# First layer's gate tiles as three pairs of seven quarter products; modulation steps four in a row

## What is computed

```python
for l in range(DEPTH):                                   # DEPTH = 2
    shift, scale, gate = jnp.split(sc @ w_ada[l] + b_ada[l], 3, axis=-1)   # modulation
    hc = rms_norm(h_ctx, norm_g[l]) * (1.0 + scale_c) + shift_c
    pc = split_cols(hc @ w_in[l])                        # context stream, layer 0
    hx = rms_norm(x, norm_g[l]) * (1.0 + scale[:, None, :]) + shift[:, None, :]
    px = split_cols(hx @ w_in[l])                        # q, k, v, gates, conv, fourier inputs
    attn = windowed_attention(q, k, v, kc, vc, attn_sink[l])
    y = jnp.concatenate([attn * silu(g_att), y_conv * silu(g_conv), y_four * silu(g_four)], -1) @ w_out[l]
    x = x + gate[:, None, :] * y
```

## Time and profile before

| | us |
|---|---|
| median of 3 runs (lowest, highest) | 1026.42 (1026.13, 1026.56) |
| profiled execution | 1026.29 |
| its span | 1024.5 |
| TensorE busy | 1000.3 (98%) |
| VectorE busy | 512.5 (50%) |
| ScalarE busy | 354.5 (35%) |
| GpSimd busy | 85.9 (8%) |
| first layer's attention | 145.65 to about 242 |

### The profile page before, as it was taken

One profiled execution on the slowest core, in us unless ns is written; L12 is line 12 of the kernel. 1 busy time (PEld: TensorE's weight loads), 2 busy tenths in 40 slices (PEclk: granted clock), 3 DMA queues, 4 the chain that ended last, 5 costly groups with the idle time before them and its releaser, 6 DMA issues.

```text
span 1024.5 us, 15340 instructions
## 1 busy us (share of the span) xinstructions
PE 1000.3 (98%) x5676; PEld 710.9 (69%) x5676; DVE 512.5 (50%) x1398; ACT 354.5 (35%) x861; POOL 85.9 (8%) x140
## 2 busy tenths in 40 slices
PE   6999999999999999999999999999999999999996
PEld 2458554556887777988999877899999744444442
DVE  5459836447365667566865824853534510000004
ACT  5224133435043247245475134742121411111113
POOL 0061000032200004300000000000000010000000
PEclk9999999999999999999999999999999999999999
DMA  9972124762233422364354352058647799999996
GB/s 362 420 303 95 42 82 178 291 272 83 83 123 130 158 83 70 130 236 139 115 202 163 126 202 83 2 195 328 237 186 307 295 396 420 419 422 420 421 419 248
DMA packets 34518, 227.57 MB, mean 222 GB/s; under 512 B 4641, under 2 KB 4913, under 8 KB 9200
## 3 DMA queue, kind: packets, MB, share of 16 engines
q1 hardware_dynamic: 31360, 214.97, 53.4%
q10 hardware_dynamic: 1920, 9.80, 2.5%
q0 software_dynamic: 1168, 1.85, 0.5%
HBM read 222.15 MB, written 8.41 MB: 225 GB/s over the span
## 4 chain that ended last, share of the span: by engine, by line
PE 90%; DVE 6%; DMA 2%; ACT 1%; issue 1%; SPq 0%; DVEq 0%; ACTq 0%
PE lin L669 12%; PE sc L686 11%; PE lin L1398 11%; PE sc L792 6%; PE aux L1398 5%; PE lin L686 4%; PE aux L1246 4%; PE sc L892 4%; PE lin L856 3%; PE sc L1363 3%; PE sc L669 3%; PE aux L922 3%; PE sc L1071 3%; PE lin L908 2%; DVE UN L2284 2%; DMA Y<-ada_in 2%
## 5 line engine op out<-in xcount | busy, mean ns | idle before, releaser
L669 PE MATMUL lin<-H,ring 128*128 128x256 f32 (+1 forms) x560 | 125.8, 385 | 0.0
L669 PEld LDWEIGHTS lin<-H,ring 128*128 128x128 f32 x560 | 106.0, 190 | 18.0 <-issue 4.2
L792 PE MATMUL sc<-H,ring 128*128 128x512 f32 (+1 forms) x192 | 67.3, 496 | 0.0
L1614 ACT ACTIVATE SP<-lin 128x512 f32<-128x512 f32 (+2 forms) x88 | 42.0, 485 | 72.7 <-PE lin L908 72.6
L2284 DVE SCALAR_TENSOR_TENSOR UN<-UN,cols 128x512 f32<-128x512 f32 (+1 forms) x120 | 66.7, 627 | 0.0
L2196 DVE CUSTOM_DVE_ANT_0 SP<-sc,CW,SK 128x512 f32<-128x512 f32 (+1 forms) x48 | 31.8, 662 | 53.6 <-PE sc L892 53.6
L1625 ACT ACTIVATE SP<-SP,ST 128x513 f32<-128x513 f32 (+4 forms) x88 | 53.8, 611 | 6.7 <-DVE ST L2199 6.4
L792 PEld LDWEIGHTS sc<-H,ring 128*128 128x128 f32 x192 | 34.8, 189 | 30.3 <-issue 25.6
L2851 DVE TENSOR_TENSOR PR<-lin,PR 128x512 f32<-128x512 f32 x8 | 5.5, 692 | 94.5 <-PE lin L1398 94.5
L892 PE MATMUL sc<-PR 64*128 64x256 f32 (+3 forms) x240 | 42.2, 434 | 2.3 <-DVE ST L2196 1.5
L1246 PE MATMUL aux<-Y,ring 128*128 128x256 f32 x192 | 42.0, 379 | 0.2 <-DVE PR L2645 0.2
(11 more groups left out here) (503 smaller groups left out, 1867.6 us busy)
## 6 DMA issues: line engine op xcount, KB each, us to landing
ring<-w_stream SPq DMA_DIRECT2D x119, 1024.0 KB, 6.7
SP<-w_stream SPq DMA_DIRECT2D x14, 1024.0 KB, 20.3
UN<-w_stream SPq DMA_DIRECT2D x10, 1024.0 KB, 18.2
PR<-w_stream SPq DMA_DIRECT2D x8, 1024.0 KB, 17.0
CW<-w_stream SPq DMA_DIRECT2D x8, 1024.0 KB, 16.4
X<-w_stream SPq DMA_DIRECT2D x8, 1024.0 KB, 18.7
Y<-w_stream SPq DMA_DIRECT2D x8, 1024.0 KB, 18.2
PR<-ada_in SPq DMA_DIRECT2D x5, 1024.0 KB, 26.4
```

The source lines that it names most:

```text
L669: m = mm(dst, w[:, k, :], rhs(k), start=n == 0, stop=n == KT - 1)
L792: m = mm(bank[:, 0:ns * SEQ], filling["w"][:, k, :], H[:, 0:ns, k, :], start=k == 0, stop=k == KT - 1)
L1614: fn(PT[:, g % TURNED, a:b], take()[:, 0:b - a], ACT.Copy).then_inc(lin_taken, 1)
```

## The change

The six gate tiles of the first layer are computed as three pairs, each by seven quarter products, as the paired tiles of the opening are. One step of the attention carries one quarter product (four products of 256 columns): 21 steps instead of 24. Each quarter lands in one of two PSUM banks by turns (`fill_bank`) and VectorE reads it there, by 9 operations of 256 columns for each pair; ScalarE's six copies are gone. A product waits until the quarter two before it has been read. The weights of a pair are one unit, which is given back after the seventh product.

The token mixtures must live on: the fourth is written to other space (where the conv's inputs stand, so after these have been used), GpSimd copies the first after its third weight mixture and the second when the last tile of both streams is done. GpSimd mixes the weights of the first gate pair before the attention, and those of the second and third ahead of the sinks of items 14 and 28. The four steps of a modulation chunk stand in a row (steps 7 to 10 and 20 to 23). The load of the kept memory moves from step 32 to 35, and `S_OUT` uses other space.

```diff
-FILLS = ([("gate", 0), ("gate", 1), ("ada", 1), ("gate", 2), ("gate", 3), ("ada", 2), ("gate", 4), ("gate", 5)],
-         [("gate", t) for t in range(GATES)])
-SEQUENCE = (("gate", 0, 0, 4), ("ada", 1, 0, 2), ("gate", 1, 0, 4), ("ada", 1, 2, 2), ("gate", 2, 0, 4), ("ada", 2, 0, 2),
-            ("gate", 3, 0, 4), ("ada", 2, 2, 2), ("gate", 4, 0, 4), ("gate", 5, 0, 4))
+FILLS = ([("ada", 1), ("ada", 2)], [("gate", t) for t in range(GATES)])
+GATE_PAIRS = GATES // 2
+SEQUENCE = (("gate", 0, 0, 7), ("ada", 1, 0, 4), ("gate", 1, 0, 7), ("ada", 2, 0, 4), ("gate", 2, 0, 7))
 GATES_FROM = ADA_BLOCKS + sum(len(f) for f in FILLS)
-PIECES = ([(what, x, 2 * q) for what, x, a, n in SEQUENCE for q in range(a, a + n)],
+PIECES = ([(what, x, q if what == "gate" else 2 * q) for what, x, a, n in SEQUENCE for q in range(a, a + n)],
           [("gate", t, 4 * q) for t in range(GATES) for q in range(2)])
-FILL_STEPS = ([*PIECES[0][:30], None, *PIECES[0][30:]],
+FILL_STEPS = ([*PIECES[0][:11], None, *PIECES[0][11:14], None, *PIECES[0][14:26], None, PIECES[0][26], None, *PIECES[0][27:]],
...
-OUT_PART, B_PART = 7 * 3, 7 * 11
+F_PART, F_ADDED, F_MIX, F_TOKENS = 7 * 3, 3 * 3, 3, 4
...
-        T_IN = [T_IN[:, q, :, :] for q in range(4)]
+        T_IN = [*(T_IN[:, q, :, :] for q in range(3)), E1[:, 1024:2048].rearrange("p (k n) -> p k n", k=4)]
+        T_FILL = [E1[:, 0:1024].rearrange("p (k n) -> p k n", k=4), H[:, 1, 0:4, :], T_IN[2], T_IN[3]]
+        S_FILL = [E1[:, QUARTER * VV:QUARTER * (VV + 1)], *(CW[:, N_C1 + QUARTER * q:N_C1 + QUARTER * (q + 1)] for q in range(2))]
         T_OUT = SP[:, 4 * 772:].rearrange("p (q k n) -> p q k n", q=3, k=4)
         T_OUT = [FT, *(T_OUT[:, q, :, :] for q in range(3))]
         T_OUT = [T_OUT, [YB[:, k:k + 4, 1, a:a + P] for k in (0, 4) for a in (0, P)]]
...
+        def fill_bank(q):
+
+            return sc[:, q % 2, 512:512 + SEQ]
+
...
+                        if layer == 0:
+                            pe.wait_ge(quarter_added, F_ADDED + 7 * GATE_PAIRS)
...
+            def gate_quarter(x, q):
+
+                n, (lo, hi), (s1, s2, s4), (t1, t3, t2, t4) = 7 * x + q, LO_HI, S_FILL, T_FILL
+                if q == 0:
+                    assert at["block"] // UNIT == FILL_UNIT[x]
+                    filling["w"] = unit_of_pair()
+                w = filling["w"]
+                if n == 0:
+                    pe.wait_ge(four_taken, 2)
+                if q == 0:
+                    pe.wait_ge(quarter_added, F_ADDED + n)
+                if q == 1 and x:
+                    pe.wait_ge(fill_taken, ADA_BLOCKS + x)
+                if q >= 2:
+                    pe.wait_ge(quarter_added, F_ADDED + n - 1)
+                if q == 0:
+                    m = quarter(fill_bank(q), w[:, 0, lo], H[:, 0, 0:4, :])
+                if q == 1:
+                    m = quarter(fill_bank(q), w[:, 0, hi], H[:, 0, 4:8, :])
+                if q == 2:
+                    pe.wait_ge(weights_mixed, 4 * (F_MIX + x) + 1)
+                    pe.wait_ge(tokens_mixed, F_TOKENS + 1)
+                    m = quarter(fill_bank(q), s1, t1)
+                if q == 3:
+                    pe.wait_ge(weights_mixed, 4 * (F_MIX + x) + 3)
+                    m = quarter(fill_bank(q), s2, t2)
+                if q == 4:
+                    pe.wait_ge(tokens_mixed, F_TOKENS + 2)
+                    m = quarter(fill_bank(q), w[:, 1, lo], t3)
+                if q == 5:
+                    pe.wait_ge(weights_mixed, 4 * (F_MIX + x) + 4)
+                    m = quarter(fill_bank(q), s4, H[:, 1, 4:8, :])
+                if q == 6:
+                    m = quarter(fill_bank(q), w[:, 1, hi], t4)
+                    at["owed"] += 1
+                m.then_inc(quarter_made, 1)
+
             def fill(layer, i):
                 ns = 2 - layer
-                if i < len(FILL_STEPS[layer]) and FILL_STEPS[layer][i]:
-                    what, x, k0 = FILL_STEPS[layer][i]
+                step = FILL_STEPS[layer][i] if i < len(FILL_STEPS[layer]) else None
+                if layer == 0 and step and step[0] == "gate":
+                    gate_quarter(*step[1:])
+                elif step:
+                    what, x, k0 = step
                     n, b, taken = fill_of(layer, what, x)
                     bank = sc[:, b, 512:1024]
                     if k0 == 0:
                         pe.wait_ge(fill_taken, taken)
-                        if n in (ADA_BLOCKS, ADA_BLOCKS + 2):
-                            pe.wait_ge(four_taken, b + 1)
+                        if layer == 0:
+                            pe.wait_ge(quarter_added, F_ADDED + 7 * x - 1)
                     if what == "ada":
                         m = ada_step(bank, k0)
                     else:
...
+                    if layer == 0 and what == "gate":
+                        return
...
-                    if layer == 0 and i == len(FILL_STEPS[0]) - 1:
-                        memory_again()
                     if i == 2 * (len(STAGES[L]) // 2):
                         act.wait_ge(fill_taken, ADA_BLOCKS + len(FILLS[0]) + layer * len(FILLS[1]))
                     for k in gate_steps.get(i, ()):
+                        if k == 4 and layer == 0:
+                            act.wait_ge(quarter_added, F_ADDED + 7 * GATE_PAIRS)
+                            memory_again()
                         if k == 4:
                             act.wait_ge(conv_norm, layer + 1)
...
+            pool.wait_ge(tokens_mixed, F_TOKENS)
+            nc.gpsimd.tensor_copy(T_FILL[0], T_IN[0]).then_inc(tokens_mixed, 1)
+            pool.wait_ge(quarter_made, F_PART)
+            pool.wait_ge(four_ready, 2)
+            mixed(F_MIX, FILL_UNIT[0], *LO_HI, S_FILL)
+            pool.wait_ge(lin_ready, turn["l0", GF + 1] + 1)
+            pool.wait_ge(tokens_mixed, F_TOKENS + 1)
+            nc.gpsimd.tensor_copy(T_FILL[1], T_IN[1]).then_inc(tokens_mixed, 1)
             pool.wait_ge(sinks_ready, 1)
+            mixed_before = {14: 1, 28: 2}
             for name in ("l0", "l1"):
                 for i, it in enumerate(STAGES[name]):
                     g = first[name] + i
+                    if g in mixed_before:
+                        x = mixed_before[g]
+                        pool.wait_ge(quarter_made, F_PART + 7 * x - 1)
...
                 layer = int(name == "l1")
                 if layer:
                     pool.wait_ge(normed["l1"], 2 * KT)
+                else:
+                    pool.wait_ge(conv_norm, 1)
+                    pool.wait_ge(roped, 5)
                 for n in range(4):
                     if n == 2:
-                        pool.wait_ge(tokens_mixed, 4 * layer + 8)
-                    mixed(len(PAIRED) + 4 * layer + n, FIRST_OUT[layer] + n, *LO_HI[::-1], S_OUT[4 * layer + n])
+                        pool.wait_ge(tokens_mixed, OUT_TOKENS + 4 * layer + 4)
...
-                    dve.wait_ge(tokens_mixed, 3)
-                    v.tensor_tensor(T_IN[3], H[:, 0, 4:8, :], T_IN[2], ALU.subtract).then_inc(tokens_mixed, 1)
...
+                if layer == 0:
+                    after(last[1])
+                    dve.wait_ge(tokens_mixed, 3)
+                    v.tensor_tensor(T_IN[3], H[:, 0, 4:8, :], T_IN[2], ALU.subtract).then_inc(tokens_mixed, 1)
...
+                def gate_quarter(x, q):
+
+                    n, added = 7 * x + q, F_ADDED + 7 * x
+                    bank, (c11, c12), (c21, c22) = fill_bank(q), *([P1[:, GA + 2 * x + f, s, :] for s in range(2)] for f in range(2))
+                    dve.wait_ge(quarter_made, F_PART + n + 1)
+                    if q == 0:
+                        v.tensor_copy(c12, bank).then_inc(quarter_added, 1)
+                    if q == 1:
+                        dve.wait_ge(quarter_added, added + 1)
+                        v.tensor_tensor(c11, c12, bank, ALU.add).then_inc(quarter_added, 1)
+                    if q == 2:
+                        v.tensor_copy(c22, bank).then_inc(quarter_added, 1)
+                    if q == 3:
+                        v.tensor_tensor(c12, c12, bank, ALU.add).then_inc(quarter_added, 1)
+                    if q == 4:
+                        dve.wait_ge(quarter_added, added + 4)
+                        v.tensor_tensor(c21, c12, bank, ALU.add).then_inc(quarter_added, 1)
+                        step(v.tensor_tensor(c12, c12, c22, ALU.add))
+                        dve.wait_ge(quarter_added, added + 5)
+                        joined_at[0] = step(v.tensor_tensor(c22, c22, c21, ALU.add))
+                    if q == 5:
+                        after(joined_at[0])
+                        v.tensor_tensor(c12, c12, bank, ALU.add).then_inc(quarter_added, 1)
+                    if q == 6:
+                        v.tensor_tensor(c21, c21, bank, ALU.add).then_inc(quarter_added, 1)
+
+                joined_at = [0]
+
                 def between(p):
+                    for i in (2 * p, 2 * p + 1):
```

(3 more changed lines are left out.)

31 lines of the change are left out of this document (18 added, 13 removed).

## The result

The changed kernel takes **1042.65 us**, median of four runs (1041.38 to 1045.08), against 1026.37 for the kernel before (1026.13 to 1026.56): a ratio of 1.0162, 95% interval 1.0143 to 1.018. The direction was predicted, the size was not: +7.3 us were forecast and +16.3 came, and 1042.65 lies 3.65 us above the range's upper end. The profiled execution is the fastest of the four (1041.38 us, span 1039.6); its span is 15.1 us longer than that of before. The trace is of that run, so the 15.1 is what can be placed.

What follows compares the result with a forecast made beforehand. TensorE was taken to bound the kernel. Gate products -5.2, ring waits +8.6 and VectorE's lateness +3.9 gave +7.3 us, so 1033.7 us, with a range of 1028.5 to 1039.

Steps and rivals of the forecast that it cites:

- What bounds the kernel: First layer: TensorE is busy 98% of the span, so each microsecond of its instructions or new waits moves the end.
- The gain of the gate products: First layer's attention: 21 quarter-product steps replace 24 gate steps, 37.4 us for 42.6, so TensorE has 5.2 us less.
- Ring waits: Attention's modulation steps, four in a row: TensorE waits for weight units, 8.6 us in sum, bounds 7.9 and 11.
- R1: Modulation steps: units are there in time, leaving -5.2 + 3.9 = -1.3 us, 1025.1 us; chance 0.08.
- The fourth mixture and the port: Before the conv: moved mixture and GpSimd's lock on the shared port make VectorE, then TensorE, 3.9 us late; bounds 1.2, 5.2.
- the rival without a lock: Before L1019, with only the fourth mixture moved: GpSimd does not hold VectorE, wait 1.5 us; no chance given.
- R2: Before L1019: VectorE's lateness does not reach TensorE, leaving -5.2 + 8.6 = +3.4 us, 1029.8 us; chance 0.14.
- R3: Neither ring waits nor VectorE's lateness cost TensorE anything, leaving -5.2 us, 1021.2 us; chance 0.05.
- What lies beside other work: Mostly attention: VectorE's 27 sums, the conv's norm, weight mixtures and ScalarE's copies put at 0, bounds -0.3 and +3 us.
- R4: Attention: VectorE's sums set the pace and each product waits for the sum two steps back, 1039 us; chance 0.11.
- The sum: Whole kernel: -5.2 + 8.6 + 3.9 = +7.3 us, which later stages keep; 1033.7 us, chance 0.62.

Runs made afterwards that it cites:

- e_turn_five: Changed kernel with early fourth mixture, modulation steps apart, units freed sooner, second modulation turn before gate sums, five useless products in step 26's ring wait: 1025.73 us.
- e_busy: Changed kernel with useless products filling TensorE's waits before L1068 and before the waiting modulation steps: 1037.42 us, ratio 1.0106 to the kernel before.

## Why the prediction was wrong, point by point

**What bounds the kernel**: right. Every wait of TensorE in the first layer, and every product less, reached the end.

**The gain of the gate products**: right, 4.9 us measured for 5.2 forecast. The forecast took the 13 groups of the kernel before for the late first product of a group; the 21 new steps stand in 18 groups, and 5 x 0.09 is the half microsecond by which 37.9 exceeds 37.4. `e_turn_five` shows that the gain is real: its attention takes 96.6 us (145.59 to 242.14) instead of 97.1, with 2.43 us of useless products and 1.6 us of ring waits in it.

**Ring waits**: right in place and size. Forecast 3.1 + 1.2 + 4.3 = 8.6; measured 3.50, 1.45 and 4.16, 9.1 in all. The unit of the first group's fourth step was said to land 6.6 us after the third step starts, 5.5 after its issue; it was issued 1.2 us after that start (176.2), as forecast, and landed 6.2 us after its issue. That of the second group was to land 5.9 us after the third step's start, and the fourth could start 6.1 us after it (221.01 to 227.09). R1 (the ring keeps up) fell. The high bound of the whole forecast, +12, holds 1 us for other work where its own bound was 3; with 3 it is 1040.4 us, still below the result.

**The fourth mixture and the port**: right. 3.9 forecast, 3.88 measured, and the split fits too: 3.12 without the copy, against 1.5 by the rival without a lock. L1019 had no slack, so R2 and R3 fell.

**What lies beside other work** (0, bounds -0.3 and +3): 0.4 in the tail's waits on ScalarE and 0.8 unplaced in the attention. No product there waits for a sum of VectorE; R4 fell, although its number, 1039, was the nearest to the result. That it was near is chance: its mechanism is not in the trace.

**The sum is the step that failed.** It adds "-5.2 + 8.6 + 3.9", each wait at its own length; that TensorE runs slower behind a wait has no term, so it was put at nothing without a reason. Behind three of the four waits the granted clock fell to 0.50, at 1.71 us each: 5.1 us in the profiled run, the largest single part of the 7.8 us between the forecast change and that of the span. `e_busy` shows that it is the idling that costs them. The others are 0.5 in the ring waits, 0.3 less gain, 0.4 in the tail, 0.4 from before the stage and 0.4 from after it, and 0.8 unplaced, less 0.1 at L1068. The median of the four runs lies 1.3 us above the profiled one, at a mean granted clock of 0.992 instead of 0.994; 0.002 of 1040 us is 2 us, so the clock can be that too, but those runs have no trace that I could place it in.

The range could not hold it, since no bound in it stood for the clock. The rows to see it were there. The earlier trace rows has the clock of the stage, 1.00, in its third number from the end; the prediction does not ask what it depends on, and the runs show that it is a result of TensorE hardly idling there. And the price of a wait can be read behind the only long one of the kernel before, that for the first load (8.7 us); PEld are TensorE's weight loads, one for each instruction:

```profile
8.72 9.27 PE L938 MATMUL lin<-ring,UN 128*128 128x512 f32 x16 [8.72 <-DMA ring<-w_stream]
...
12.29 0.34 PEld L938 LDWEIGHTS lin<-ring,UN 128*128 128x128 f32 x1 [0.52 <-issue]
...
13.54 0.19 PEld L938 LDWEIGHTS lin<-ring,UN 128*128 128x128 f32 x1 [0.24 <-issue]
```

Up to 12.29 us the weight loads take 0.34 us and stand 0.86 apart, from 13.11 on they take 0.19 and stand 0.43 apart. The 16 instructions need 9.1 us until the next one starts (17.82), where at 0.43 each they would need 6.9: 2.2 us lost. The clock column says 1.00 there, so this is read from the pace and not from the column; but where the column says 0.50 in the changed kernel, behind L1068, the weight loads take the same 0.34 us.

The Trainium skill (TensorE: Matmul & The Clock Gate, on the oscillation in real kernels) describes this loss for waits on a DMA between bursts of products, and counts it as half of the time at the lower rate. The runs agree: stretches of about 3.4 us at half clock, 1.7 us lost each. They add that a wait on VectorE does the same (L1068).

## What to carry to other kernels

Where the trace shows the clock at full rate through a stage, price each new wait of TensorE of about 2 us and more at its length plus the half clock behind it (here 1.7 us, sometimes 2.9). Keep new waits short: none of 1.68 us or less brought the half clock here. To test whether a loss is the wait or the clock, fill the wait with products that nobody reads: they must fit inside it, so measure one first. Saved work is worth nothing until the operands of what moves up arrive as early: here 4.9 us of saved products needed the mixture, the modulation steps and the turn moved, and idle products, to show at all, and then by 0.1%.
